# Padding that moves operand tiles of four product stages, and the first stage's turning of tiles put inside the product

## The chip, the cores and the metric

One Trainium2 chip; the kernel runs on one of its cores. The metric is the device time of one execution in microseconds (us). The kernel before was run three times: 4549.24, 4552.47 and 4555.07 us, median 4552.47. One execution was also profiled.

## The reference

Two transformer blocks of different build follow each other on 1024 tokens of width 1024, in float32. Only the dense products matter here; what stands between them (gated linear attention, windowed attention, retention, a delta rule, long convolutions) is left out.

```python
# first block
h = layer_norm(x) * (1.0 + scale1) + shift1
proj = h @ w_in[l]                                  # 1024 x 6416 weights
x = layer_norm_affine(ALPHA * x + gate1 * (y @ w_o[l]), ln1_g[l], ln1_b[l])
h2 = layer_norm(x) * (1.0 + scale2) + shift2
u = h2 @ w_up[l]                                    # 1024 x 5632
f = jax.nn.gelu(u_gate, approximate=False) * u_val
x = layer_norm_affine(ALPHA * x + gate2 * (f @ w_down[l]), ln2_g[l], ln2_b[l])
# second block, layer 0 (even), on 1024 tokens and 256 of context
u_l = h_l @ w_in                                    # 1024 x 4352
u_c = h_c @ w_in
# second block, layer 1 (odd)
u_l = h_l @ w_in                                    # 1024 x 4096
kv_c = h_c @ w_in[:, O_NK:O_NZ]
```

## The kernel before

The program is a chain of stages, in this order: g_in (first projection, with windowed attention and the modulation rows woven in), gla, proj1, up, down, g_even, ret, prep, rwkv, proj2, g_odd, mix, proj3. Each stage (`stage`, L44) gives back its memory and semaphores at its end. Within a stage each engine has its own instruction stream, written out by hand; semaphores tie them together.

Every float32 product is done as three products of rounded parts: each operand is split into a high part (an ACT copy into F32R) and a low part (a DVE subtraction), and high x high, high x low and low x high are summed in PSUM. One product instruction has a stationary operand of 128x128 and a moving one of 128x512 (the last strip is narrower). In g_in, g_even and g_odd the helper `gemm_units` (L84) does it: a unit is one strip of 512 weight columns times one tile of 128 tokens, 8 chunks of 128 input features x 3 = 24 matmuls (`multiply`, L139; L151 to L153); activations `hi`, `lo` are stationary, weights `w_hi`, `w_lo` moving. Weight chunks are loaded by SP's queue into `raw`, a ring of 4 (`load`, L118), split by ACT (L131) and DVE (L137) into a ring of `slots` chunks, and the last four chunks of the next strip wait for the last unit of this one. PSUM has two banks, emptied by ACT and DVE in turn (L167, L173), and POOL's queue stores the results (L178). In up (L1592) it is the other way round: weights stationary, activations moving, 22 column blocks x 96 matmuls. In down (L1835 to L1839) the activations `f_hi`, `f_lo` are stationary and the weights moving; blocks of 36 matmuls (24 in the last pass) take their weights in turn from three places: for two of three blocks from spare columns of `hi`, `lo` (shown as h_hi, h_lo), for the third from `w_hi2`, `w_lo2` (shown as down_w_hi, down_w_lo). In the proj stages (L468 to L470) activations `y_hi` are stationary and weights moving.

A memory tile of a stage stands right behind the one opened before it, rounded up to 32 bytes of each partition; so shapes give every tile's place. The 128x128 identity comes first (512 bytes), then the activations of the stage. Counted within 512 bytes from the identity's first byte, the operands of the products stand at:

| stage | activations | weights | tiles in between whose size is no multiple of 512 bytes |
|---|---|---|---|
| g_in | 0 | 0 | none |
| proj1 | 96 | 96 | (`mod_cols1`, 96 bytes, before both) |
| up | 0 | 288 | `mod_cols1` 96, `taps` 704 |
| down, two blocks of three | 192 | 0 | `mod_cols` 192, before f_hi |
| down, third block | 192 | 192 | |
| g_even | 0 | 192 | `mod_cols` 192 |
| proj2 | 192 | 192 | |
| g_odd | 0 | 192 | `mod_cols2` 192 |
| proj3 | 0 | 0 | |

The start of g_in. `in_order` (L1086) is run by every engine with its own functions. A tile of x is loaded by POOL's queue into one of two buffers (`x_in`, L1075), its moments are taken and it is scaled into `xn` by DVE (`norm`, L1382 to L1398, with ACT's square root L1348 in between); PE turns it with eight 128x128 transposes into `pt` (L1273); ACT scales and shifts it from `pt` into `h` (eight activations, L1357) and copies the high part (L1360); DVE subtracts for the low part (L1411). There is one `xn`, one `pt` and one `h`, so the tiles go through one at a time. The order is norm(0), norm(1), turn_in(0), and then for each unit u: norm(u+2), turn_in(u+1), unit(u), the attention steps from unit 24 on and the modulation rows from unit 4 on. Unit u waits for the low part of tile u (`h_lo`, L1286 to L1287); the transposes of tile u+1 stand ahead of unit u on PE and wait until ACT has emptied `pt` of tile u. Before that, PE sums the first eight modulation blocks (L1259) as their loads land, and DVE makes `cols` from them (L1403 to L1408) right after the low parts of the first eight weight chunks.

Of the kernel before, what the change touches and what calls it, by code (L numbers as in the profile page):

```python
# [17 lines left out]
P = 128  # L18
# [51 lines left out]
RAW = 4  # L70
# [13 lines left out]
def gemm_units(s, sb, ps, hi, lo, w, strips, plan, slots=12):  # L84
# [3 lines left out]
    raw = sb("g_raw", [P, RAW, width])  # L88
# [50 lines left out]
    def multiply(pe, u):  # L139
# [6 lines left out]
        for k in range(KC):  # L146
            c = st * KC + k
# [868 lines left out]
def in_stage(nc, ident, t_eye, padded, src, w_first, b_first, w_in, P1, pos, sinks, t_mask, t_first, t_freq, YB, conds, mods):  # L1016
# [5 lines left out]
    with stage(nc, "g_in", "id_in", "zero", "pad_out", "c_in", "c_silu", "f0", "f1", "f2", "f3", "f4", "f5", "f6", "f7", "bias_T", "row_mm", "rows", "cond", "silu", "rows_in", "cols_T", "cols", "in_even", "in_odd", "var", "std", "xn", "in_T", "h", "h_hi", "h_lo",  # L1022
# [52 lines left out]
        x_in = sc[:].rearrange("p a h k -> p a (h k)")  # L1075
# [10 lines left out]
        def in_order(norm, turn_in, unit, step, mod):  # L1086
# [24 lines left out]
        def _(sp):  # L1111
# [48 lines left out]
            in_order(lambda t: None, lambda t: None, unit, step, mod)  # L1160

        @block.gpsimd
        def _(pool):
            def load_in(t):
                if t >= 2:
                    pool.wait_ge(s.xn, t - 1)
                if t < NT:
                    pool.dma_start(x_in[:, t % 2], src[t * P:(t + 1) * P, :]).then_inc((s.in_even, s.in_odd)[t % 2], DMA)
            load_in(0)
            load_in(1)  # L1170
# [23 lines left out]
            in_order(lambda t: load_in(t + 1) if t else None, lambda t: None, unit, step, mod)  # L1194
# [6 lines left out]
        def _(pe):  # L1201
# [61 lines left out]
            def turn_in(t):  # L1263
# [21 lines left out]
            def unit(u):  # L1285
# [4 lines left out]
                gemm.multiply(pe, u)  # L1290
# [9 lines left out]
            in_order(lambda t: None, turn_in, unit, step, mod)  # L1300

        @block.scalar
        def _(act):
# [42 lines left out]
            def norm(t):  # L1346
                act.wait_ge(s.var, t + 1)
                act.activation(rstd[:, 0:1], rstd[:, 1:2], ACT.Sqrt).then_inc(s.std, 1)  # L1348

            def turn_in(t):  # L1350
                act.wait_ge(s.in_T, t + 1)
                if t == 0:
                    act.wait_ge(s.cols, 1)
                else:
                    act.wait_ge(s.h_lo, t)
# [17 lines left out]
            def first(t):  # L1373
                norm(t)
                if t == 1:
                    for c in range(KC):
                        gemm.split_hi(act, c)
# [2961 lines left out]
```

## Time and profile before

| | us |
|---|---|
| median of three runs | 4552.47 (4549.24 to 4555.07) |
| the profiled execution | 4550.96 |
| its span from first to last instruction | 4549.2 |
| PE busy with matmuls | 4064.8 (89%) |
| DVE busy | 2600.8 (57%) |
| ACT busy | 1481.1 (33%) |
| mean granted TensorE clock | 0.936 |

The sections below read the same trace in more detail. A duration of a matmul holds its fill and drain and overlaps the next one; what a matmul costs in a stream is the distance from one start to the next. Times in the trace count from the span's start.

### The profile page before, as it was taken

Reading aid. Unit: us, or ns where it says so; the run is one execution under the profiler, and the core shown is the slowest. Engines: PE = TensorE matmul, PEld = TensorE weight load, DVE = VectorE, ACT = ScalarE, POOL = GpSimd, SP = SyncE. Lnnn points to the kernel's source line nnn. Section 1 sums busy time; section 2 is a strip of 40 time slices with the busy share of each in tenths; the row PEclk is TensorE's granted clock in tenths of the full one; section 3 lists DMA queues with packets and bytes.
Section 4 is the critical chain, followed back from the end, with each engine's and each line's share of the span. In section 5 each row is a group of like instructions: output and inputs, shape, how many; then the busy total and the mean of one; then the engine's idle time right before and its main releaser. Section 6 shows DMA issues by size and latency. Waiting matters only on the chain. (4 is left out here: it accounts for less than half of the span.)

```text
span 4549.2 us, 71258 instructions
## 1 busy us (share of the span) xinstructions
PE 4064.8 (89%) x27486; PEld 3117.6 (69%) x27486; DVE 2600.8 (57%) x4923; ACT 1481.1 (33%) x3051; POOL 614.4 (14%) x802
## 2 busy tenths in 40 slices
PE   6999999768999989799997577899968999989988
PEld 4877776557888877588886233788766778755647
DVE  4567775667333348711237686777765335465746
ACT  4223232734222235411104243334433311143423
POOL 1111111000000000010123012000010013333320
PEclk8999999889999999899997688999878999999999
DMA  6544433542111144522323585444434335453334
GB/s 203 185 149 138 160 128 112 182 145 92 46 46 47 36 134 154 165 94 86 116 105 113 171 304 205 122 115 133 113 98 151 134 117 193 162 159 97 105 97 158
DMA packets 422564, 599.56 MB, mean 132 GB/s; under 512 B 166703, under 2 KB 279811, under 8 KB 419621
## 3 DMA queue, kind: packets, MB, share of 16 engines
q1 hardware_dynamic: 369037, 417.99, 29.8%
q0 software_dynamic: 51120, 174.80, 10.5%
q8 instruction: 204, 3.34, 0.3%
q10 hardware_dynamic: 2088, 2.49, 0.2%
q14 instruction: 115, 0.94, 0.1%
HBM read 430.45 MB, written 164.71 MB: 131 GB/s over the span
## 5 line engine op out<-in xcount | busy, mean ns | idle before, releaser
L151 PE MATMUL g_in_g_acc<-g_in_g_whi,g_in_hi 128*128 128x512 f32 (+1 forms) x832 | 328.7, 395 | 5.7 <-DVE g_in_lo L1411 5.7
L152 PE MATMUL g_in_g_acc<-g_in_g_wlo,g_in_hi 128*128 128x512 f32 (+1 forms) x832 | 319.0, 383 | 0.0
L153 PE MATMUL g_in_g_acc<-g_in_g_whi,g_in_lo 128*128 128x512 f32 (+1 forms) x832 | 318.6, 383 | 0.0
L151 PE MATMUL g_even_g_acc<-g_even_g_whi,h_hi 128*128 128x512 f32 (+1 forms) x720 | 276.4, 384 | 12.4 <-DVE g_even_g_wlo L137 12.4
L152 PE MATMUL g_even_g_acc<-g_even_g_wlo,h_hi 128*128 128x512 f32 (+1 forms) x720 | 275.7, 383 | 0.0
L153 PE MATMUL g_even_g_acc<-g_even_g_whi,h_lo 128*128 128x512 f32 (+1 forms) x720 | 275.5, 383 | 0.0
L1668 DVE SCALAR_TENSOR_TENSOR rows<-up_acc,up_taps,rows 128x1023 f32<-128x1023 f32 x88 | 112.8, 1282 | 284.4 <-ACT rows L1643 277.1
L1592 PE MATMUL up_acc<-h_hi,up_w_hi 128*128 128x512 f32 x704 | 225.6, 397 | 13.1 <-DVE up_w_lo L1682 11.1
L151 PE MATMUL g_odd_g_acc<-g_odd_g_whi,h_hi 128*128 128x512 f32 x544 | 218.5, 402 | 17.0 <-DVE g_odd_g_wlo L137 11.4
L1592 PE MATMUL up_acc<-h_lo,up_w_hi 128*128 128x512 f32 x704 | 225.3, 397 | 0.0
L1592 PE MATMUL up_acc<-h_hi,up_w_lo 128*128 128x512 f32 x704 | 225.1, 397 | 0.0
L152 PE MATMUL g_odd_g_acc<-g_odd_g_wlo,h_hi 128*128 128x512 f32 x544 | 216.7, 398 | 0.0
L153 PE MATMUL g_odd_g_acc<-g_odd_g_whi,h_lo 128*128 128x512 f32 x544 | 216.6, 398 | 0.0
L1436 DVE SCALAR_TENSOR_TENSOR g_in_m_acc<-g_in_m_w,g_in_c_act,g_in_m_acc 128x256 f32<-128x256 f32 x448 | 202.0, 482 | 22.3 <-issue 0.4
L151 PEld LDWEIGHTS g_in_g_acc<-g_in_g_whi,g_in_hi 128*128 128x128 f32 x832 | 156.5, 188 | 66.0 <-issue 26.0
L468 PE MATMUL proj_acc<-proj_w_hi,proj_y_hi 128*128 128x512 f32 x416 | 170.7, 410 | 15.2 <-DVE proj_w_lo L543 15.2
L153 PEld LDWEIGHTS g_in_g_acc<-g_in_g_whi,g_in_lo 128*128 128x128 f32 x832 | 156.6, 188 | 31.5
L152 PEld LDWEIGHTS g_in_g_acc<-g_in_g_wlo,g_in_hi 128*128 128x128 f32 x832 | 156.8, 188 | 27.4
L1643 ACT ACTIVATE rows<-up_acc,up_taps 128x1024 f32<-128x1024 f32 x44 | 53.1, 1206 | 372.1 <-PE up_acc L1592 372.1
L470 PE MATMUL proj_acc<-proj_w_hi,proj_y_lo 128*128 128x512 f32 x416 | 166.1, 399 | 0.0
L469 PE MATMUL proj_acc<-proj_w_lo,proj_y_hi 128*128 128x512 f32 x416 | 166.0, 399 | 0.0
L151 PEld LDWEIGHTS g_even_g_acc<-g_even_g_whi,h_hi 128*128 128x128 f32 x720 | 135.7, 188 | 43.6 <-DVE g_even_g_wlo L137 14.0
(640 smaller groups left out, 9450.8 us busy)
## 6 DMA issues: line engine op xcount, KB each, us to landing
rest<-in_w_down SPq DMA_DIRECT2D x66, 512.0 KB, 3.6
g_in_g_raw<-in_w_in SPq DMA_DIRECT2D x96, 256.0 KB, 4.1
P<-g_in_g_o POOLq DMA_DIRECT2D x96, 256.0 KB, 2.7
g_in_m_w<-in_ada_w SPq DMA_DIRECT2D x24, 1024.0 KB, 5.4
up_w_buf<-in_w_up SPq DMA_DIRECT2D x42, 512.0 KB
U<-g_even_g_o POOLq DMA_DIRECT2D x80, 256.0 KB, 2.3
g_odd_x<-U3p SPq DMA_DIRECT2D x24, 768.0 KB, 6.9
g_in_m_w<-in_w_ada SPq DMA_DIRECT2D x16, 1024.0 KB, 6.4
```

Of the source, the lines that this page charges most:

```text
L151: pe.matmul(bank[:, :wd], hi[:, k, tt], w_h, start=k == 0, stop=False)
L152: pe.matmul(bank[:, :wd], hi[:, k, tt], w_l, start=False, stop=False)
L153: op = pe.matmul(bank[:, :wd], lo[:, k, tt], w_h, start=False, stop=k == KC - 1)
L468: pe.matmul(acc[t % 2][hf][:], y_hi[:, t % 2, k, :], w_hi[:, k, cs], start=k == 0, stop=False)
L469: pe.matmul(acc[t % 2][hf][:], y_hi[:, t % 2, k, :], w_lo[:, k, cs], start=False, stop=False)
L470: op = pe.matmul(acc[t % 2][hf][:], y_lo[:, t % 2, k, :], w_hi[:, k, cs], start=False, stop=k == KC - 1)
L1436: dve.scalar_tensor_tensor(acc, w, c_act[:, k, c:c + 1], acc, ALU.mult, ALU.add)
L1592: op = pe.matmul(acc[par][side][:, tt], wt[:, par, side, k, :], ht[:, k, tt], start=k == 0 and wt is w_hi and ht is hi, stop=k == KC - 1 a ...
L1643: act.activation(cv[:, side], acc[par][side][:], ACT.Identity, scale=taps[:, 2, col], bias=taps[:, 3, col]).then_inc(s.act_c, 1)
L1668: dve.scalar_tensor_tensor(cv[:, side, lag:], acc[par][side][:, :SEQ - lag], taps[:, tap, col], cv[:, side, lag:], ALU.mult, ALU.add)
```

## The change

Four edits of memory layout and one of order. (1) `gemm_units` takes `pad`; `raw` gets `width + pad` columns per chunk. g_even and g_odd pass 20, so `raw` is 4 x 20 x 4 = 320 bytes longer. (2) `taps` in up gets 14 more columns in each of its 4 rows, 224 bytes. (3) down opens an unused tile `place` of 320 bytes ahead of `f_hi`. With these the operands of up, down, g_even and g_odd stand at the same place within 512 bytes (0, 0, 0 and 0). The chunks of `raw` then begin 2128 bytes apart in place of 2048. (4) In g_in the turning of tile u+2 moves into unit u, after 12 of its 24 matmuls (`middle`); x tiles have three buffers (the third is `y`, unused so early) and `norm` is cut in `moments` and `scale`, run one and two tiles further ahead; the moments of tile 2 come ahead of the making of `cols`, and POOL issues the loads of tiles 0 to 2 at once, tile 3 after the scaling of tile 0, tiles 4 and 5 ahead of the first store.

```diff
-def gemm_units(s, sb, ps, hi, lo, w, strips, plan, slots=12):
+def gemm_units(s, sb, ps, hi, lo, w, strips, plan, slots=12, pad=0):
-    raw = sb("g_raw", [P, RAW, width])
+    raw = sb("g_raw", [P, RAW, width + pad])
...
-    def multiply(pe, u):
+    def multiply(pe, u, middle=None):
...
         for k in range(KC):
+            if k == KC // 2 and middle:
+                middle()
...
-        x_in = sc[:].rearrange("p a h k -> p a (h k)")
+        x_in = [sc[:, 0].rearrange("p h k -> p (h k)"), sc[:, 1].rearrange("p h k -> p (h k)"),
+                y[:].rearrange("p h d -> p (h d)")]
+        x_done = (s.in0, s.in1, s.in2)
...
-            norm(0)
-            norm(1)
-            turn_in(0)
+            for what, t in (("moments", 0), ("scale", 0), ("moments", 1), ("scale", 1), ("chunks", 0), ("moments", 2), ("turn", 0), ("low", 0),
+                            ("turn", 1), ("scale", 2), ("moments", 3), ("low", 1)):
+                early(what, t)
             for u in range(gemm.units):
-                if u + 2 < NT:
-                    norm(u + 2)
-                if u + 1 < NT:
-                    turn_in(u + 1)
+                for what, t in (("turn", u + 2), ("scale", u + 3), ("moments", u + 4), ("low", u + 2)):
+                    if t < NT:
+                        early(what, t)
                 unit(u)
...
             def load_in(t):
-                if t >= 2:
-                    pool.wait_ge(s.xn, t - 1)
-                if t < NT:
-                    pool.dma_start(x_in[:, t % 2], src[t * P:(t + 1) * P, :]).then_inc((s.in_even, s.in_odd)[t % 2], DMA)
-            load_in(0)
-            load_in(1)
+                if t >= 3:
+                    pool.wait_ge(s.xn, t - 2)
+                pool.dma_start(x_in[t % 3], src[t * P:(t + 1) * P, :]).then_inc(x_done[t % 3], DMA)
+            for t in range(4):
+                load_in(t)
...
-            in_order(lambda t: load_in(t + 1) if t else None, lambda t: None, unit, step, mod)
+            in_order(lambda what, t: load_in(t + 3) if what == "scale" and 1 <= t < NT - 3 else None, unit, step, mod)
...
-                gemm.multiply(pe, u)
+                gemm.multiply(pe, u, (lambda: turn(u + 2)) if u + 2 < NT else None)
...
-            in_order(lambda t: None, turn_in, unit, step, mod)
+            in_order(lambda what, t: turn(t) if what == "turn" and t < 2 else None, unit, step, mod)
...
+            def early(what, t):
+                if what == "moments":
+                    act.wait_ge(s.var, t + 1)
+                    act.activation(rstd[:, 0:1], rstd[:, 1:2], ACT.Sqrt).then_inc(s.std, 1)
+                if what == "chunks":
+                    for c in range(KC):
+                        gemm.split_hi(act, c)
...
+                if what == "low":
+                    act.activation(hi[:, :, rows(t * P)], h, ACT.Copy).then_inc(s.h_hi, 1)
...
-        taps = sb("taps", [P, 4, 2 * FC])
+        taps = sb("taps", [P, 4, 2 * FC + 14])
...
-                dve.tensor_copy(taps[:, c, :], acc[1][0][:, c * P:c * P + 2 * FC])
+                dve.tensor_copy(taps[:, c, :2 * FC], acc[1][0][:, c * P:c * P + 2 * FC])
...
+        sb("place", [P, 80])
         f_hi = sb("f_hi", [P, W_BUF, 384], F32R)
...
-        gemm = gemm_units(s, sb, ps, hi, lo, w_in, EVEN_STRIPS, plan)
+        gemm = gemm_units(s, sb, ps, hi, lo, w_in, EVEN_STRIPS, plan, pad=20)
...
-        gemm = gemm_units(s, sb, ps, hi, lo, w_in, ODD_STRIPS, plan, slots=10)
+        gemm = gemm_units(s, sb, ps, hi, lo, w_in, ODD_STRIPS, plan, slots=10, pad=20)
```

ACT's and DVE's functions of the first stage are cut along the same names; `turn` keeps the eight activations L1357, `low` has the copy L1360 and the subtraction L1411, `scale` has L1391 to L1398, `moments` L1384 to L1390.

## Rows read from the trace of the kernel before

**Rows 1.** Busy time by stage: length, busy us per engine, clock, DMA share, GB/s.
```profile
1610.00:1895.00 285.00, 256.89 (x1120) 207.54 (x1120) 198.39 (x378) 134.18 (x285) 11.75 (x17) 0.97 0.51 158
1895.00:2395.00 500.00, 482.62 (x2178) 391.45 (x2179) 126.33 (x205) 68.57 (x122) 73.77 (x134) 0.98 0.31 106
3570.00:3985.00 415.00, 397.08 (x1657) 312.09 (x1657) 163.84 (x143) 65.23 (x109) 112.90 (x101) 0.98 0.46 161
```

**Rows 2.** The same view, PE alone: within g_even, g_odd, up.
```profile
1940.00:2300.00 360.00, 360.00 (x1544) 1.00 0.29 98
3750.00:3880.00 130.00, 130.00 (x559) 1.00 0.55 195
1130.00:1600.00 470.00, 470.00 (x2016) 1.00 0.15 43
```

**Rows 3.** Timeline of PE in g_in: start, length, operation; 29 and 23 distances.
```profile
101.04 0.39 PE L152 MATMUL g_in_g_acc<-g_in_g_wlo,g_in_hi 128*128 128x512 f32 x1
...
107.64 0.39 PE L151 MATMUL g_in_g_acc<-g_in_g_whi,g_in_hi 128*128 128x512 f32 x1
...
112.85 0.39 PE L153 MATMUL g_in_g_acc<-g_in_g_whi,g_in_lo 128*128 128x512 f32 x1
```

**Rows 4.** Timeline of PE in proj2; 24 distances lie between the two.
```profile
3465.74 0.39 PE L468 MATMUL proj_acc<-proj_w_hi,proj_y_hi 128*128 128x512 f32 x1
...
3471.18 0.39 PE L468 MATMUL proj_acc<-proj_w_hi,proj_y_hi 128*128 128x512 f32 x1
```

**Rows 5.** Timeline of PE in down: between the rows 17 and 36 distances.
```profile
1624.97 0.39 PE L1836 MATMUL down_acc<-down_w_lo,down_f_hi 128*128 128x512 f32 x1
...
1628.82 0.40 PE L1835 MATMUL down_acc<-h_hi,down_f_hi 128*128 128x512 f32 x1
...
1637.08 0.40 PE L1835 MATMUL down_acc<-down_w_hi,down_f_hi 128*128 128x512 f32 x1
```

**Rows 6.** Timeline of PE, narrow strips: g_even (46 distances), g_in (29).
```profile
2359.83 0.28 PE L151 MATMUL g_even_g_acc<-g_even_g_whi,h_hi 128*128 128x256 f32 x1
...
2365.04 0.28 PE L152 MATMUL g_even_g_acc<-g_even_g_wlo,h_hi 128*128 128x256 f32 x1
...
154.26 0.29 PE L152 MATMUL g_in_g_acc<-g_in_g_wlo,g_in_hi 128*128 128x272 f32 x1
...
157.90 0.29 PE L151 MATMUL g_in_g_acc<-g_in_g_whi,g_in_hi 128*128 128x272 f32 x1
```

**Rows 7.** Timeline of PE in g_in: units 0, 1, 3 and transposes.
```profile
47.41 0.79 PE L151 MATMUL g_in_g_acc<-g_in_g_whi,g_in_hi 128*128 128x512 f32 x1 [0.37 <-DVE g_in_lo L1411]
...
54.59 1.03 PE L1273 MATMUL g_in_pt<-ident,g_in_pT 128*128 128x128 f32 x8
55.38 0.47 PE L151 MATMUL g_in_g_acc<-g_in_g_whi,g_in_hi 128*128 128x512 f32 x1
...
70.72 0.50 PE L151 MATMUL g_in_g_acc<-g_in_g_whi,g_in_hi 128*128 128x512 f32 x1 [1.24 <-DVE g_in_lo L1411]
...
77.21 1.06 PE L1273 MATMUL g_in_pt<-ident,g_in_pT 128*128 128x128 f32 x8 [0.76 <-ACTq L1358]
```

**Rows 8.** Groups by line, 0:111: count, busy us, mean ns, idle before.
```profile
L1357 ACT ACTIVATE g_in_pT<-g_in_pt,g_in_cols 128x128 f32<-128x128 f32 x64 | 23.2, 467 | 4.3 <-DVEq L1408 2.9 <-DVE g_in_lo L1411 1.4
L1411 DVE TENSOR_TENSOR g_in_lo<-g_in_pT,g_in_hi 128x1024 fp32r<-128x1024 f32 x8 | 9.8, 1225 | 23.7 <-ACT g_in_hi L1360 23.7
L1360 ACT ACTIVATE g_in_hi<-g_in_pT 128x1024 fp32r<-128x1024 f32 x8 | 8.5, 1058 | 0.8
```

**Rows 9.** Timeline of DVE around the first unit.
```profile
39.77 0.68 DVE L1403 COPY g_in_x<-g_in_pm 128x512 f32<-128x512 f32 x1
...
47.28 1.28 DVE L1386 BATCH_NORM_STATS2 g_in_stats<-g_in_sc 128x6 f32<-128x512 f32 x2
...
48.93 0.15 DVE L1390 TENSOR_SCALAR g_in_rstd<-g_in_mv 128x1 f32<-128x1 f32 x1
```

**Rows 10.** Busy time of 20:40; columns as in rows 1.
```profile
20.00:40.00 20.00, 6.87 (x32) 0.76 (x32) 8.00 (x16) 4.74 (x9) 7.01 (x10) 0.59 1.02 309
```

More of the change, by code:

```diff
@@ L1159, in _ @@
                 gemm.load(sp, c)
-            in_order(lambda t: None, lambda t: None, unit, step, mod)
+            in_order(lambda what, t: None, unit, step, mod)
         @block.gpsimd
@@ L1371, in unit, with moments @@
                 gemm.evacuate_act(act, u)
[L1373 to L1377, printed above, removed]
-            in_order(lambda t: first(t) if t < 2 else norm(t), turn_in, unit, step, lambda m: None)
+            in_order(early, unit, step, lambda m: None)
         @block.vector
         def _(dve):
-            def norm(t):
-                xt = x_in[:, t % 2]
-                dve.wait_ge((s.in_even, s.in_odd)[t % 2], (t // 2 + 1) * DMA)
+            def moments(t):
+                dve.wait_ge(x_done[t % 3], (t // 3 + 1) * DMA)
                 for hf in range(2):
-                    dve.bn_stats(stats[:, hf, :], xt[:, hf * 512:(hf + 1) * 512])
+                    dve.bn_stats(stats[:, hf, :], x_in[t % 3][:, hf * 512:(hf + 1) * 512])
                 dve.drain()
@@ new lines, in early @@
+            def early(what, t):
+                if what == "moments":
+                    if t == 0:
+                        dve.memset(zeros, 0.0).then_inc(s.zero, 1)
+                    if t == 1:
+                        dve.wait_ge(s.bias_T, 1)
+                        dve.tensor_copy(cols[:], bias_T)
+                    moments(t)
+                if what == "scale":
+                    scale(t)
+                    if t == 0:
+                        dve.memset(ones[:], 1.0)
+                if what == "chunks":
+                    for c in range(KC):
+                        gemm.split_lo(dve, c)
+                if what == "turn" and t == 0:
+                    columns()
+                if what == "low":
+                    dve.wait_ge(s.h_hi, t + 1)
+                    dve.tensor_tensor(lo[:, :, rows(t * P)], h, hi[:, :, rows(t * P)], ALU.subtract).then_inc(s.h_lo, 1)
@@ L1524, in unit @@
                 gemm.evacuate_dve(dve, u)
-            def first(t):
-                if t == 0:
-                    dve.memset(zeros, 0.0).then_inc(s.zero, 1)
-                if t == 1:
-                    dve.wait_ge(s.bias_T, 1)
-                    dve.tensor_copy(cols[:], bias_T)
-                norm(t)
-                if t == 0:
-                    dve.memset(ones[:], 1.0)
-                if t == 1:
-                    for c in range(KC):
-                        gemm.split_lo(dve, c)
-            in_order(lambda t: first(t) if t < 2 else norm(t), turn_in, unit, step, mod)
+            in_order(early, unit, step, mod)
 def ffn_up_stage(nc, ident, hi, lo, left, cols, X1, cv, w_up, conv_w, conv_b, fT):
```

54 lines of the change are left out of this document (24 added, 30 removed).

## The prediction

> **What bounds the kernel now.** I began with the busy time by stage. In down, g_even and g_odd PE works 257 of 285, 483 of 500 and 397 of 415 us, DVE 198, 126 and 164, and the DMA share is 0.51, 0.31 and 0.46 [rows 1]. Inside them and inside up the same view shows stretches of 360, 130 and 470 us in which PE has no gap at all, at a granted clock of 1.00, which is the 2.4 GHz level [rows 2]. So these stages last as long as PE needs for their matmuls, and a change in the distance from one matmul to the next goes straight into the end. The length printed at a matmul (0.39) is no help there, as it overlaps the next; the distance is a stretch divided by its matmuls.
>
> That distance is not the same in all stages. Of the count in a stretch one or two only reach into it. g_even: 360 us over 1543 is 233.3 ns; up: 470 over 2015 is 233.3; g_odd: 130 over 558 is 233.0 [rows 2]. g_in needs 5.21 us for 23, 226.5 ns, and 11.81 us for 29 + 23 = 52, 227.1, over a stretch that has a few slower distances in it [rows 3]. proj2 needs 5.44 for 24, 226.7 [rows 4]. The table of places orders them: g_in and proj2 have both operands at one place within 512 bytes (0 and 0, 192 and 192), the slow three are 192 or 288 bytes apart. It is the distance of the places and not the weights' own place: in proj2 and in g_even the weights stand at 192 alike. Nor is it the roles, since up has them exchanged. Down has both kinds in one stage, with the same instructions: its third block, both operands at 192, needs 3.85 us for 17, 226.5, and the following 36 matmuls, 192 bytes apart, 8.26 us, 229.4 [rows 5]. That is the strongest row for the change, and also a warning: in down the price of being apart is 2.9 and not 6.7 ns.
>
> **Part 1, the places.** Nothing is added to any engine; 320, 224, 320 and 320 bytes of memory are. I take 227.1 as the distance after, the value with slower distances in it, and 233.3 before, so 6.2 ns a matmul; 6.8 would be the bound above (233.3 to 226.5), 0 the bound below unless the rival decides.
> - g_even: 8 strips of 512 columns x 10 token tiles x 24 = 1920 matmuls x 6.2 = 11.9 us.
> - g_odd: 68 units x 24 = 1632 x 6.2 = 10.1 us.
> - up: 22 x 96 = 2112 x 6.2 = 13.1 us.
> - down: 22 x (18 + 18 + 12) = 1056 x (229.4 - 227.1) = 2.4 us. The third blocks gain as well, because the row at 226.5 is the first of its kind and later ones start out of a block that is apart; but in the last two passes DVE is close behind (198 busy of 285 over the stage) [rows 1], so I take 1.5.
> - g_even's last strip has 256 columns: 240 matmuls. Apart they need 5.21 us for 46, 113.3 ns. The nearest row at one place is g_in's strip of 272: 3.64 us for 29, 125.5, or 118.1 for 256 columns in proportion [rows 6]. So the narrow strip may lose 240 x 4.8 = 1.2 us; I take all of it. Its bound below is 0.
>
> Sum 11.9 + 10.1 + 13.1 + 1.5 - 1.2 = 35.4 us. It is on the path since PE is the bound; the cover of the other engines is large (DVE 126 of 500 in g_even). What is late next in each stage is what is late now: the first weight chunks at its start.
>
> The rule of the Trainium skill that speaks against this is in "TensorE: Matmul & The Clock Gate", Part 2, step 1 of the walk through a matmul: loading the next stationary operand "doesn't steal SBUF read bandwidth from the running matmul", as each has its own read port. By it the place could not matter and part 1 would be worth 0. The rows disagree, as the same instruction form runs at 226.5 and at 229.4 in one stage [rows 5]; still it is a rival below. The same page's figure for a matmul of 512 columns in a row, about 216 ns, is under every row here, so both levels carry a cost that it lacks.
>
> The chunks of `raw` now begin at multiples of 16 bytes that are no multiples of 64. The trace shows no DMA to such a place. Its bound below is a gain of 0, since nothing in it gets shorter; above, if each load took half as long again, only the first chunks of g_even and g_odd would show, some 2 us each; later chunks are loaded a strip ahead and a strip lasts 56 or 45 us. I take 0 and keep 4 in the range.
>
> **Part 2, the first stage.** Removed from the path: the wait for `h_lo` ahead of units 3, 4, 5 and 6 and the wait for `pt` ahead of transposes, 1.24 and 0.76 at the rows shown [rows 7], and the drains and starts around them. Kept: the transposes themselves, 0.79 us from 54.59 to 55.38, and a slower first matmul behind each (0.47 to 0.50 against 0.39) [rows 7], about 0.1. Eight units now take 47.41 to 107.64, 60.2 us [rows 7, 3]. After: unit 0 has its first matmuls at the lower clock level as now (0.79 long against 0.39) [rows 7]: from 47.41 to 54.59 are 7.2, plus 0.8 and some 0.1 for transposes: 8.1. Units 1 to 5: 24 x 0.2268 = 5.44, plus 0.9: 6.35 each, 31.8. Units 6 and 7 hold no transposes: 10.9. Sum 50.8, so 9.4 less.
>
> This holds if the chain of the other engines fits in a unit of 6.35. ACT needs 2.9 for the eight activations and 1.06 for the copy, DVE 1.2 for the low part [rows 8], 5.2 in a row per tile, since `h` is single; beside them DVE takes the moments (1.8) [rows 9] and the scaling, which it does while ACT works. Before unit 4 this leaves about a unit's length as slack, because the low part of tile u+2 is due only after unit u+1. From unit 4 on DVE has the modulation rows as well, but no more moments. The tightest places are the transposes in unit 4 and the start of unit 5, with about 1 us each by this count; a miss costs what it misses, up to 2 us.
>
> Two things are moved ahead of the first unit. The moments of tile 2 stand between the last weight chunk and the making of `cols` on DVE: 47.28 to 49.08 is 1.8 us for the same work [rows 9]. Behind them in DVE's queue is L1403, now right at the chunk's end (39.77) [rows 9], for which PE, ACT and so the first unit wait. So +1.8. And POOL's queue issues the loads of x tiles 2 to 4 before that point, where tile 4 (0.5 MB) came behind the first unit's store before; the DMA engines are full there (share 1.02 between 20 and 40 us, 309 GB/s) [rows 10], so the last weight chunk lands later by 0.5 MB over 309 GB/s, 1.7 us. I take that; the bounds are 0 and 3, as earlier loads of tiles 2 and 3 could also hold up tile 1 and the first chunks. POOL's constants behind these loads are due much later. SP's loads of modulation weights stand behind a chunk that DVE splits after the low part of tile 3, some 5 us later than now, and are wanted only in unit 4.
>
> Sum of part 2: 9.4 - 1.8 - 1.7 = 5.9 us, from 2 to 9.5. From unit 8 on the stage runs as before, PE without waits, so the shift goes through.
>
> **The sum.** The profiled execution took 4551.0 with a span of 4549.2, 1.5 under the median of the runs. 4551.0 - 35.4 - 5.9 = 4509.7, stated as 4510; were the median of its runs 1.5 above it again, it would be 4511.
>
> **The rivals.**
> - Only part of the places helps. Down shows 2.9 ns where the others show 6.7, so what decides may be a pattern of places and order, and up (moving activations, each stationary tile used twice) has no sister at one place. Without up: 4510 + 13 = 4523; with half the gain everywhere, 4528. Against it: four streams at one place, in three stages and two shapes of loop, all give 226.5 to 227.1.
> - The places do nothing (the rule above, or the distance comes of something else that these stages share, such as the longer rows of `hi` in g_even and g_odd). Then part 2 alone is left: 4551 - 6 = 4545, and it is "the same" by the bound below. Against it: up has the short rows and is slow; down has both in one stage.
> - Slower: at one place the load of the stationary tile and the stream collide, and the 226.7 of g_in comes from elsewhere. Being apart would be the better place, as it is in the narrow strips (118 against 113 ns) [rows 6]. If the wide ones lost the same 4.8 ns, 6720 matmuls x 4.8 = 32 us, less 6: 4577. It decides if the loss sits in the load of 128 columns whatever the stream's width. Against it: proj2's and g_in's wide streams.
> - The first stage gives nothing because the start comes later than counted: 4510 + 6 = 4516, inside the range.
>
> **How the numbers follow.** Forecast, including a first stage of 2 to 9.5: 0.83. Part of the places: 0.08. Nothing: 0.05. Slower: 0.03; a mixture between nothing and slower: 0.01. Faster by over 0.2% (9 us, about what a measurement of this kernel can tell from no change) is 0.92 with a share of the partial cases, the same 0.05, slower 0.03. Low end: 6.8 in place of 6.2 ns (3.4 us), no loss in the narrow strip (1.2), 9.5 in the first stage (3), less a little: 4502. High end: 2 in the first stage (4), 4 for `raw`, and up to the partial cases: 4524.
>
> **What would show it.** In the changed profile the stretches of g_even, g_odd and up should hold 2.8% more matmuls each (360 us: 1587 and not 1544); up's stage should end 13 us sooner after its start; down's blocks of all three kinds should run at 226.5 to 227.5. Unit 0 of g_in should start at 51, unit 8 at 102, with no wait for L1411 between. Wrong would be: a distance still at 233 with both operands at one place; PE waits for `w_lo` at strip changes; L1403 later than 43.

## The result, and the profile after

The changed kernel took 4517.9 us in the median of four executions (4514.4 to 4523.1), the kernel before beside it 4552.9 (4549.2 to 4555.1): a ratio of 0.9923, 95% interval 0.9908 to 0.9939. It is faster by about 35 us; forecast were 41, counted from the profiled execution of 4551.0. The time lies inside the range of 4502 to 4524 and 8 us above the forecast of 4510. The profiled execution took 4514.4 us with a span of 4512.6, which is 36.6 less than the span before, at the same mean granted clock (0.937 and 0.936).

Stage by stage, from the first matmul of a stage to its last:

| stage | before | after | change | forecast |
|---|---|---|---|---|
| g_in, to its end | 778.4 | 772.8 | -5.6 | -5.9 |
| up | 498.8 | 485.1 | -13.7 | -13.1 |
| down | 274.2 | 272.1 | -2.1 | -1.5 |
| g_even | 488.7 | 477.0 | -11.7 | -10.7 |
| g_odd | 403.9 | 399.0 | -4.9 | -10.1 |
| all the rest, by difference | | | +1.4 | 0 |

The view of PE alone in stretches without a gap answers to [rows 2]; columns as there.

```profile
1920.00:2280.00 360.00, 360.00 (x1590) 1.00 0.31 104
1120.00:1580.00 460.00, 460.00 (x2031) 1.00 0.16 44
3860.00:3930.00 70.00, 70.00 (x311) 1.00 0.44 155
```

g_even holds 1590 matmuls in 360 us where it held 1544: 360 / 1589 = 226.6 ns. up: 460 / 2030 = 226.6. g_odd: 70 / 310 = 225.8, one matmul more or less being 0.7 ns. So the distances came down by the full 6.7 ns and not by the 6.2 of the forecast. Counted from unit to unit, each unit of 24 matmuls is 0.16 us shorter, in g_even's wide strips from the fifth unit on and in up from the second of its 22 column blocks on without exception.

The narrow strip went the other way. Timeline of PE in g_even after, 46 distances between the two, against 5.21 us for as many before [rows 6]: 5.52 us, 120.0 ns.

```profile
2325.58 0.28 PE L156 MATMUL g_even_g_acc<-g_even_g_whi,h_lo 128*128 128x256 f32 x1
...
2331.10 0.28 PE L154 MATMUL g_even_g_acc<-g_even_g_whi,h_hi 128*128 128x256 f32 x1
```

The start of g_in, timelines of PE and of DVE, against [rows 7] and [rows 9]:

```profile
42.81 1.12 PE L1285 MATMUL g_in_pS<-ident,g_in_x 128*128 128x128 f32 x4 [6.07 <-DVE g_in_x L1405]
...
49.70 0.79 PE L154 MATMUL g_in_g_acc<-g_in_g_whi,g_in_hi 128*128 128x512 f32 x1 [0.37 <-DVE g_in_lo L1432]
...
100.53 0.39 PE L154 MATMUL g_in_g_acc<-g_in_g_whi,g_in_hi 128*128 128x512 f32 x1
```
```profile
38.49 1.95 DVE L138 TENSOR_TENSOR g_in_g_wlo<-g_in_g_raw,g_in_g_whi 128x512 fp32r<-128x512 f32 x3 [0.47 <-ACT g_in_g_whi L132]
40.36 1.28 DVE L1387 BATCH_NORM_STATS2 g_in_stats<-g_in_y 128x6 f32<-128x512 f32 x2
...
42.07 0.68 DVE L1405 COPY g_in_x<-g_in_pm 128x512 f32<-128x512 f32 x1
```

Unit 0 starts at 49.70 and not 47.41, unit 8 at 100.53 and not 107.64: eight units in 50.83 us. The 7.11 us won by then are still there to 0.01 at unit 76; at unit 80 they are 5.54. In between the granted clock fell to the lower level for about 3.4 us, which shows as a mean of 0.89 in this stretch, beside 1.00 in the same one before (PE busy, clock, DMA share, GB/s; before is the first):

```profile
560.00:575.00 15.00, 13.43 (x81) 1.00 0.41 158
```
```profile
560.00:575.00 15.00, 13.43 (x79) 0.89 0.26 89
```

And g_odd has a wait that was nearly absent before. Waits of PE there, 3700 to 3960 before, then 3700 to 3920 after (total, times, longest):

```profile
PE g_odd_g_acc L151 <- DVE g_odd_g_o L173: 5.6, 1, 5.6
PE g_odd_g_acc L151 <- DVE g_odd_g_wlo L137: 1.1, 1, 1.1
```
```profile
PE g_odd_g_acc L154 <- DVE g_odd_g_o L176: 5.5, 2, 5.3
PE g_odd_g_acc L154 <- DVE g_odd_g_wlo L138: 4.3, 1, 4.3
```

The second line, the wait for `w_lo`, is in the first unit of a strip, at its seventh matmul. Counted from 0 as in g_in this is unit 52; the expectations below call it unit 53. Ahead of it nearly every unit of g_odd is 0.16 us shorter than before; across it 4.5 us of that are lost: 3.2 in the longer wait, the rest in matmuls at the lower clock level right behind it (the clock is 0.89 over 3845:3860 and 1.00 over the 70 us after).

### The profile page after: what moved, and what is told of

Its sections match the earlier page's. It is cut to its first block and busy times, and to the rows that moved or that the text cites. A ratio compares the mean times of both kernels' runs of the same rounds, so it can differ in the third digit from the quotient of the medians.

```text
span 4512.6 us, 71257 instructions
## 1 busy us (share of the span) xinstructions
PE 4035.5 (89%) x27486; PEld 3123.9 (69%) x27486; DVE 2607.0 (58%) x4923; ACT 1480.6 (33%) x3051; POOL 614.2 (14%) x802
## 5 line engine op out<-in xcount | busy, mean ns | idle before, releaser
L154 PEld LDWEIGHTS g_even_g_acc<-g_even_g_whi,h_hi 128*128 128x128 f32 x720 | 136.4, 189 | 39.0 <-DVE g_even_g_wlo L138 14.1
```

What stands on the lines that cost most here:

```text
L154: pe.matmul(bank[:, :wd], hi[:, k, tt], w_h, start=k == 0, stop=False)
```

## Where the wait in g_odd comes from

DVE runs the convolution of a tile between its other duties. In the last unit of a strip (unit 51 here) its queue holds the low parts of the next strip's last six weight chunks: six and not four as in g_in and g_even, because g_odd's ring has ten places. A tile's first product stands ahead of them. Timelines of DVE and of POOL after, then the same place before:

```profile
3846.36 1.82 DVE L3655 SCALAR_TENSOR_TENSOR g_odd_x<-g_odd_x,g_odd_edges,g_odd_w 128x1536 f32<-128x1536 f32 x1 [10.16 <-DMA g_odd_x<-U3p]
3848.25 5.55 DVE L138 TENSOR_TENSOR g_odd_g_wlo<-g_odd_g_raw,g_odd_g_whi 128x512 fp32r<-128x512 f32 x4
3846.41 5.04 POOL L3587 TENSOR_TENSOR g_odd_x<-g_odd_x,g_odd_w 128x1536 f32<-128x1536 f32 x1 [4.00 <-DMA g_odd_x<-U3p]
```
```profile
3880.60 1.82 DVE L3645 SCALAR_TENSOR_TENSOR g_odd_x<-g_odd_x,g_odd_edges,g_odd_w 128x1536 f32<-128x1536 f32 x1 [6.13 <-DMA g_odd_x<-U3p]
3882.49 5.65 DVE L137 TENSOR_TENSOR g_odd_g_wlo<-g_odd_g_raw,g_odd_g_whi 128x512 fp32r<-128x512 f32 x4
3880.84 4.94 POOL L3577 TENSOR_TENSOR g_odd_x<-g_odd_x,g_odd_w 128x1536 f32<-128x1536 f32 x1
```

The same work of the same length; but unit 52, the first that needs these low parts, started at 3884.77 before and at 3846.19 after. So x landed 4.2 us ahead of that unit before, and 0.2 behind its start after. DVE stands in the wait for x with the low parts behind it. A second delay follows from the same landing: POOL starts its own product of the tile then, and the first of the four low parts (one row above) takes 3.75 us beside it (3.84 before) where the others take 0.68. It ends at 3852.00, and PE's wait at 3852.05. Before, this delay was as long, but the low parts had started early enough to hide most of it. Without it PE would have waited about 1.2 us and not 4.3, by an estimate from 3.75 and 0.68. The timeline of SP says why x is late in terms of units: its loads are issued when DVE has finished the tile before,

```profile
3871.06 1.27 SPq L3529 DMA_DIRECT2D g_odd_x<-U3p  x3
```
```profile
3835.17 1.28 SPq L3539 DMA_DIRECT2D g_odd_x<-U3p  x3
```

which is 13.7 us ahead of unit 52 before and 11.0 after, and they took 9.5 us from issue to DVE's release before and 11.2 after. The chain finish, load, first product has its own length in us; the steps that hold it are counted in units, and the units became shorter. Each tile's load waits for the tile before, so the lag adds up over the tiles. That was the reading of the two traces; the runs below test it.

## The experiments

Ratios are against the kernel before on the same chip. Distances are the mean of all start-to-start distances of a stage's wide matmuls under 300 ns, unless a row is shown; in down they are those of the two blocks of three whose relative place the padding changes. Line numbers of each kernel are its own.

**Each part alone.** The first kernel is the kernel before with the padding only, the second the changed kernel without it (the line is that of g_even and g_odd; `taps` in up and `place` in down likewise):

```diff
-        raw = sb("g_raw", [P, RAW, width])
+        raw = sb("g_raw", [P, RAW, width + 20])
```

> The kernel before with only the memory padding of up, down, g_even and g_odd, the first stage untouched. Theory A (the distance between matmuls is set by the places of the two operands within 512 bytes, 233.3 ns apart and 226.7 at one place, whatever the first stage does): every unit of 24 matmuls is 0.16 us shorter, up 14 us shorter, g_even 11, down 2, g_odd 11 less a wait for w_lo at a strip change of 4, in all 31 to 34 us: 4519 to 4522. Rival B (part of the gain of these stages comes of the shifted start of everything, that is of the moments at which loads and clock changes fall): under 25 us, 4528 or more.

Measured: 4524.6 us against 4556.4, ratio 0.9934 (0.9918 to 0.9951), 32 us less, which is inside theory A's 31 to 34 and far from rival B's 25. up 486.2 long, down 272.4, g_even 477.5, g_odd 400.8, all within 2 us of the changed kernel; g_in as before.

> The changed first stage alone, all tiles at their former places. Theory A: unit 0 of g_in starts near 49.7 and unit 8 near 100.5, 7.1 us ahead of before, and all later stages run at 233.3 ns as before; 7 us less, or 5.5 if the clock falls once within g_in as it did in the changed kernel: 4545 to 4547. Rival: the clock's fall near 565 us is an accident of one execution and is not seen here (then 4545); or it follows from the earlier start (then the fall is there again at 560 to 570).

Measured: 4545.7 against 4556.4, ratio 0.9980 (0.9971 to 0.9990), 11 us less by the medians; in its trace unit 8 of g_in starts at 100.74 and the stage ends at 771.5, 6.9 us ahead of before, all of it kept, since the clock did not fall inside the stage. up, g_even and g_odd run at 233.3 ns. The parts add up within their intervals: 0.9934 x 0.9980 = 0.9914, against 0.9923 for both. Waits of PE in g_odd, with the padding alone and with the first stage alone:

```profile
PE g_odd_g_acc L151 <- DVE g_odd_g_wlo L137: 5.6, 1, 5.6
```
```profile
PE g_odd_g_acc L154 <- DVE g_odd_g_wlo L138: 0.4, 1, 0.4
```

The wait at the strip change goes with the padding and not with the earlier start. It remains to tell the shorter units from raw's odd places.

**raw at multiples of 2048 again.**

```diff
-    raw = sb("g_raw", [P, RAW, width + pad])
+    if pad:
+        sb("g_place", [P, 80])
+    raw = sb("g_raw", [P, RAW, width])
```

> The changed kernel, but the 320 bytes in g_even and g_odd are an unused tile ahead of raw, so that raw's chunks are 2048 bytes apart as before and not 2128; the operands stand at the same places as in the changed kernel. Theory A (the odd places of raw's chunks cost nothing; the wait for w_lo at the strip change in g_odd comes of DVE standing in a wait for a tile of the convolution): g_odd keeps its wait of 3 to 5 us at unit 53, total as the changed kernel, 4517 within 2. Rival B (loads to places that are no multiples of 64 bytes, or reads from them, are slower and cause that wait): the wait is gone or under 1.5 us and the total is 3 to 5 us less, 4513.

Measured: 4520.1, ratio 0.9919 (0.9903 to 0.9936). The wait is there in full:

```profile
PE g_odd_g_acc L156 <- DVE g_odd_g_wlo L140: 5.4, 1, 5.4
```

So raw's places cost nothing that these runs can tell, rival B falls, and the 4 us kept for them above the forecast were not needed.

**DVE's first convolution product one step later.**

```diff
-                if n == 0:
+                if n == 1:
                     dve.wait_ge(s.const, 5 * DMA)
                     dve.wait_ge(s.x_in, (t + 1) * (3 * DMA))
                     dve.scalar_tensor_tensor(before, before, edges[:, 0, t:t + 1], w[:, 0], ALU.mult, ALU.mult)
                     dve.drain()
-                if n == 1:
                     dve.scalar_tensor_tensor(behind, behind, edges[:, 1, t:t + 1], w[:, 2], ALU.mult, ALU.mult)
```

> The changed kernel, with one change in g_odd: DVE does the first product of a convolution tile (the one that waits for the three loads of x) one step later, together with the second, so that some 3.6 us more lie between the loads' issue and the wait. Theory A (the new wait of PE at unit 53 is DVE's queue: it stands in the wait for x, 10.16 us there, and the low parts of the next strip's last four chunks stand behind it): DVE no longer waits there, PE's wait of 4.34 goes under 1, g_odd ends 3 to 4.4 us sooner, 4513.5 to 4515 on the scale on which the changed kernel is 4517.9. Rival B (the low parts are late because POOL multiplies beside them, 4.4 us for one in place of 0.69): POOL still starts when x has landed, so a wait of 2 to 4 us stays.

Measured: 4511.9, ratio 0.9902 (0.9884 to 0.9919); g_odd 392.4 us long instead of 399.0 and, in a second execution of the changed kernel, 399.9. Timeline of DVE at the same strip change:

```profile
3843.23 2.73 DVE L138 TENSOR_TENSOR g_odd_g_wlo<-g_odd_g_raw,g_odd_g_whi 128x512 fp32r<-128x512 f32 x4 [6.11 <-ACT g_odd_g_whi L132]
3849.86 2.20 DVE L138 TENSOR_TENSOR g_odd_g_wlo<-g_odd_g_raw,g_odd_g_whi 128x512 fp32r<-128x512 f32 x2 [3.90 <-ACT g_odd_g_whi L132]
3851.98 0.68 DVE L176 COPY g_odd_g_o<-g_odd_g_acc 128x512 f32<-128x512 f32 x1
3852.59 1.80 DVE L3655 SCALAR_TENSOR_TENSOR g_odd_x<-g_odd_x,g_odd_edges,g_odd_w 128x1536 f32<-128x1536 f32 x1
```

The low parts come at their time, the convolution behind them without a wait. PE's waits in 3700:3920:

```profile
PE g_odd_g_acc L154 <- DVE g_odd_g_wlo L138: 3.8, 5, 1.6
PE g_odd_g_acc L154 <- DVE g_odd_g_o L176: 2.4, 2, 1.9
```

At unit 52 PE now waits 0.2 us for low parts and not 4.3, as theory A has it (under 1). Theory A's 3 to 4.4 us for the stage were too small: the wait of 5.3 us for `g_odd_g_o`, which is in the kernel before too (5.6), had the same cause (in the changed kernel's trace DVE waits 12.01 us for the first tile's x, with the emptying of a PSUM bank behind it) and shrinks to 1.9. But the edit moves waits too: 3.6 of the 3.8 us above stand in the first units of strips that had no wait before (units 34, 44 and 60). The two kinds together are 6.2 us where they were 9.8; the clock gives the rest, a mean of 0.98 over these 220 us in the changed kernel and of 1.00 here. In the three later kernels that hold this edit the waits sum to 6.2 to 6.6 us.

Rival B expected a wait of 2 to 4 us to stay at unit 52, and none did. Yet the run doesn't clear POOL: the edit takes the low parts out of the wait for x and out of POOL's product at once, as they are done at 3845.96 and POOL starts at 3847.41. Four low parts took 5.55 us beside POOL's product and 2.73 here. So that DVE's wait for x is what made the wait of PE grow is shown, since POOL's delay was in the kernel before too; how the 4.3 us divide between the two is read from the trace alone. No run leaves DVE's product in its place and moves POOL's.

**Which places are good.** Three kernels with other paddings, raw unpadded. A number is the place of the moving operand less that of the stationary one within 512 bytes; the edit is the size of the padding only.

> The changed kernel with other places: moving minus stationary operand within 512 bytes is 192 in g_in (0 in the changed kernel), 256 in g_even, 64 in g_odd, 128 in up and 64 in two of three blocks of down. Theory A1 (only the same place within 512 bytes is fast): all five run at 233.3, g_in loses 15 us over 96 wide units. Theory A2 (the same place within 256 bytes is enough, as of two halves): g_even at 226.7, the others at 233.3. Theory A3 (within 64 bytes): refuted already, since 192 is slow; if 64 or 128 were fast here the distance would count and not the place within a row. g_in at 192 must become slow by every theory that has the place as the cause; if g_in stays at 226.7, the cause lies in the other stages' code.

> More places, moving minus stationary within 512 bytes: 32 in g_in, 384 in g_even, 320 in g_odd, 96 in up, 192 in two blocks of three of down. Theory A (what counts is the difference within 256 bytes, with a cost that grows from 0 at 0 over 2.4 ns at 64 and 5.7 at 128 to 6.7 at 192): g_even at 384 runs as at 128, 232.4; g_odd at 320 as at 64, 229.1; g_in at 32 near 228; up at 96 near 231; down at 192 near 233. Theory B (256 is a second good place, but within 512 each difference has its own cost): g_odd at 320 or g_even at 384 differ by over 1 ns from that.

> More places, moving minus stationary within 512 bytes: 160 in g_in, 32 in g_even, 448 in g_odd, 256 in up and 256 in two blocks of three of down. Theory A (difference within 256 bytes): up and down run at 226.7 to 227.3 as at one place; g_odd at 448 as at 192, 233.3; g_even at 32 near 228; g_in at 160 near 233. Theory B as in the run before: up at 256 slow, since its stationary operands are the weights, or g_odd at 448 off by over 1 ns. For the narrow strip of 256 columns, 120.0 ns at a difference of 0 and 256 and 113.4 at 192, theory A gives a value in between at 32.

Measured, with the kernels before and after for 0, 192, 224 and down's 320 (g_in's means hold the work between its matmuls: 228.2 at one place, so 5.0 to 6.0 are the price there). The three kernels ran once each, 4543.5, 4552.4 and 4545.1 us; their distances are what counts here:

| difference within 512 | within 256 | ns per wide matmul |
|---|---|---|
| 0 | 0 | up, g_even 226.7; g_odd 227.0; down 227.2; g_in 228.2 |
| 256 | 0 | up, g_even 226.7; down 227.1 |
| 32 | 32 | g_even 233.3; g_in 233.2 |
| 64 | 64 | g_odd 229.1; down 229.4 |
| 320 | 64 | g_odd 230.0; down 229.6 |
| 96 | 96 | up 233.4 |
| 128 | 128 | up 232.4 |
| 384 | 128 | g_even 232.4 |
| 160 | 160 | g_in 234.2 |
| 192 | 192 | g_even, g_odd, g_in, down 233.3 |
| 448 | 192 | g_odd 233.4 |
| 224 | 224 | up 233.4 |

The stretches without a gap, PE alone (in g_even's rows of the first two kernels the products only, without the transposes that fall into them). Difference 256 in g_even, 128 in up (first kernel):

```profile
1940.00:2300.00 360.00, 359.37 (x1586) 1.00 0.30 101
1130.00:1590.00 460.00, 460.00 (x1981) 1.00 0.15 45
```

384 in g_even, 96 in up (second); 32 in g_even, 256 in up (third):

```profile
1940.00:2300.00 360.00, 359.37 (x1547) 1.00 0.28 98
1130.00:1590.00 460.00, 460.00 (x1974) 1.00 0.16 45
```
```profile
1940.00:2300.00 360.00, 360.00 (x1545) 1.00 0.30 102
1130.00:1590.00 460.00, 460.00 (x2031) 1.00 0.17 46
```

What follows. The place is the cause: g_in, fast before and after, became slow when its weights were set 192 bytes off, with its code unchanged; it took 777.0 us and not 765, of which about 1.6 are a fall of the clock. The same place within 256 bytes is enough: 256 is as good as 0 in three stages, 384 equals 128, 448 equals 192, and 320 equals 64 within 1 ns (230.0 and 229.1 in g_odd, just under theory B's bound of 1). The price does not grow with the difference, as theory A of the second and third kernel had it: 32 costs the full 6.7, 64 only 2.4 to 3.3, 128 again 5.7. The two roles are alike (up has its weights stationary). And the wait for low parts in the last part of g_odd goes with the length of a unit: at 233.3 and 233.4 ns 1.1, 0.4 and 0, at 230.0 1.1, at 229.1 2.5, at 227.0 4.3 to 5.6 us.

One thing in the kernel before doesn't fit a price that is set by the place alone. In down the third block of three (18 matmuls; the 36 of [rows 5] are two blocks) has both operands at one place, and the prediction read 226.5 ns from the first of them. The other 21 took 227.4 to 231.3 in the mean, as the second, timeline of PE before:

```profile
1637.08 0.40 PE L1835 MATMUL down_acc<-down_w_hi,down_f_hi 128*128 128x512 f32 x1
...
1639.40 0.62 PE L1839 MATMUL down_acc<-down_w_hi,down_f_lo 128*128 128x512 f32 x2
...
1641.21 0.40 PE L1835 MATMUL down_acc<-h_hi,down_f_hi 128*128 128x512 f32 x1
```

The first ten distances take 2.32 us, 232 ns each, the last eight 1.81 us, 226 each. So behind a block whose operands stand apart, a stream at one place needs about ten matmuls to reach its level; where PE had waited just before, it needed fewer in most cases. With all blocks at one place, in the changed kernel, 15 of 22 third blocks run at 226.6 to 226.7 from their first distance on. The sweeps gave all blocks of up, g_even and g_odd one place, so their means don't hold this.

**The moments of tile 2 behind the making of cols.**

```diff
-("chunks", 0), ("moments", 2), ("turn", 0), ("low", 0),
+("chunks", 0), ("turn", 0), ("moments", 2), ("low", 0),
```

> The changed kernel, with the moments of tile 2 behind the making of cols and not ahead of it. Theory A (unit 0 is late by these 1.7 us on DVE): DVE takes the sums at 40.4 instead of 42.07, unit 0 starts at 48.0 instead of 49.70 and everything behind it 1.7 us sooner; DVE then works on the moments while ACT makes h, and nothing waits for them. Rival B (the modulation sums on PE are not ready before 42, so that the moments cost nothing): start unchanged at 49.7. Rival C: the moments then push the low part of tile 0, start at 49 or later.

Its profiled execution took 12321 us at a mean granted clock of 0.41, which nothing in this edit explains and no other run shows, so its trace isn't used. The timed ones took 4511.6 to 4520.5, ratio 0.9907 (0.9887 to 0.9927), which doesn't tell 1.7 us from nothing. The edit is read from the next kernels, which hold it too.

**The changed kernel again, and three edits together.** The third edit, in `gemm_units`, moves a narrow strip's weights within their chunk:

```diff
+    def cols_of(wd):
+        at = 48 if wd < width else 0
+        return slice(at, at + wd)
...
-            w_h, w_l = w_hi[:, c % slots, :wd], w_lo[:, c % slots, :wd]
+            w_h, w_l = w_hi[:, c % slots, cols_of(wd)], w_lo[:, c % slots, cols_of(wd)]
```

> The changed kernel once more, beside the next one on the same chip, to see which of the differences between two executions belong to the kernel. Theory A: distances, the wait of PE at unit 53 of g_odd (4 to 5.5 us) and unit 0 of g_in at 49.7 come again; the fall of the clock inside g_in at 565 us does not, so that g_in ends 1.6 us sooner, at 771. Ratio to the kernel before 0.992.

Measured: 4520.2, ratio 0.9927 (0.9913 to 0.9940), span of the profiled execution 4512.7. Unit 0 at 50.02, unit 8 at 100.14, g_in's end at 770.8 and no fall of the clock within it; the wait at the strip change in g_odd is 5.4. All as expected.

> The changed kernel with three edits that each undo a loss seen in it: DVE's first convolution product one step later in g_odd, the moments of tile 2 behind the making of cols, and the last, narrow strip's weights 192 bytes on within their chunk in gemm_units (g_even's 256 columns, g_in's 272). Theory: g_odd 4 to 6.5 us shorter; unit 0 of g_in at 48.0 and not 49.7, in all 1.7; the narrow strip of g_even back at 113.4 ns and not 120.0, 240 x 6.6 = 1.6 us, g_in's 272 columns at 123.4 and not 125.3, 192 x 1.9 = 0.4. Sum 8 to 10 us less than the changed kernel, ratio to the kernel before 0.990. Rivals: without the moments' share (unit 0 stays at 49.7 because PE's sums are late anyway) 6.5 to 8.5; if the narrow strip's place does not decide its distance, it stays at 120.0.

Measured: 4509.0, ratio 0.9902 (0.9887 to 0.9916), 11 us less than the changed kernel beside it by the medians and 7.4 by the profiled spans. g_odd is 393.9 long, 6.0 less, which is most of it. Timelines of DVE and PE at g_in's start:

```profile
39.26 1.97 DVE L141 TENSOR_TENSOR g_in_g_wlo<-g_in_g_raw,g_in_g_whi 128x512 fp32r<-128x512 f32 x3 [0.27 <-ACT g_in_g_whi L135]
41.14 0.69 DVE L1408 COPY g_in_x<-g_in_pm 128x512 f32<-128x512 f32 x1
```
```profile
48.87 0.80 PE L157 MATMUL g_in_g_acc<-g_in_g_whi,g_in_hi 128*128 128x512 f32 x1 [0.46 <-DVE g_in_lo L1435]
```

The sums follow the last chunk at once, so the 1.7 us between them are gone as theory A of the moments has it; but the chunk itself is 0.8 us later in this execution, so that unit 0 starts 0.8 to 1.2 sooner and not 1.7 (48.87 here, 48.68 and 48.70 in the two kernels below). g_in ends no earlier (770.9), because the clock fell for 3.4 us at 702, which costs the 1.6 us again. And the narrow strip disappoints: g_in's 272 columns run at 123.4 as expected, g_even's 256 at 117.8 and not 113.4. As late_step alone has the same ratio, 0.9902, the times can't tell whether the other two edits are worth anything.

**The narrow strip.** Two kernels ask why. In the first `at` is 176 (704 bytes) and not 48. In the second the narrow strips are not moved; all of g_in's weights stand 512 bytes further on, and g_even's 512 bytes further than in the kernel before.

> As the kernel with the three edits, but the narrow strip's weights stand 704 bytes on within their chunk and not 192: the same place within 512 bytes, another within 1024. There the 256 columns took 117.8 ns at 192 bytes and not the 113.4 of the kernel before, whose weights stood 192 within 512 from the activations too, but 512 bytes elsewhere within 1024. Theory A (for a narrow stream the place within 1024 bytes counts): 113.4 here, g_even 1.1 us shorter. Theory B (what the distance settles into depends on the strips before it, which ran at one place here and apart in the kernel before): 117.8 again.

> The three-edit kernel without the shift of the narrow strips; instead all weights of g_in stand 512 bytes further on (difference 0 within 512) and those of g_even 512 bytes further than in the kernel before (difference 192). Theory for the wide strips: only the place within 256 bytes counts, so g_in's wide ones keep 228.2 in the mean with what is between them and g_even's run at 233.3. For the narrow strip of g_even, theory A (place within 1024 bytes): 117.8; theory B (the strips before it): 113.4 as in the kernel before, since wide strips apart go before it here as there.

Measured, as 46 distances of the narrow strip each, timelines of PE in g_even of the first and of the second: 5.42 us, 117.8 ns; 5.22 us, 113.5 ns.

```profile
2329.97 0.28 PE L159 MATMUL g_even_g_acc<-g_even_g_whi,h_lo 128*128 128x256 f32 x1
...
2335.39 0.28 PE L157 MATMUL g_even_g_acc<-g_even_g_whi,h_hi 128*128 128x256 f32 x1
```
```profile
2343.04 0.28 PE L158 MATMUL g_even_g_acc<-g_even_g_whi,h_lo 128*128 128x256 f32 x1
...
2348.26 0.28 PE L156 MATMUL g_even_g_acc<-g_even_g_whi,h_hi 128*128 128x256 f32 x1
```

Theory A, the place within 1024 bytes, is refuted twice. Both results agree with theory B, that the distance depends on the strip before it (apart: 113.4; at one place: 117.8 with its own weights apart, 120.0 with them at one place). Two earlier kernels speak against it in this simple form. In the third kernel of the sweep all of g_even stood 32 bytes apart, wide strips (233.3) and narrow one alike, and the narrow one took 117.8; its expectation had asked for a value between 113.4 and 120.0. The second kernel, 128 bytes apart within 256, gave 118.7. And g_in's 272 columns, 192 bytes apart, took the same 125.7 in the mean behind wide strips at one place (the three edits) and behind wide strips 192 bytes apart (first kernel of the sweep), against 127.6 at one place. What a strip takes over from what ran before is seen in down, above, but there it is gone after ten matmuls; what sets the narrow strips' distance stays open. The wide strips did as their theory says: g_in 228.2 with the 512 bytes, g_even 233.3. The first kernel took 4513.9, ratio 0.9906 (0.9889 to 0.9922), the second 4523.1 in one execution. Neither is better than the three edits with 48 (0.9902), nor are those better than late_step alone (0.9902).

## Why the prediction held, and where it was off

- The distance is set by the relative place, in every stage and both roles: right, and shown by g_in's loss at 192 bytes. What in the chip makes the difference no run here shows. The size was a little low. I took 227.1 for the distance after, a value with slower distances in it; it is 226.7, so 6.67 ns a matmul and not 6.2. up 88 x 0.16 = 14.1 (13.1 taken), g_even 80 x 0.16 = 12.8 (11.9), g_odd 68 x 0.16 = 10.9 before its wait (10.1).
- Down. The row called the strongest, 226.5 in the third block, was the one such block of 22 in its stage that ran so; the others give 227.4 to 231.3 with the same places. The forecast took this into account ("later ones start out of a block that is apart"), but as evidence for the place the row was luck; what carries the claim is g_in. The warning row, 229.4 in place of 233.3 [rows 5], has its reason: 320 bytes apart is 64 within 256, and 64 is a half-good place in g_odd too (229.1, 230.0). 2.1 us came, of 1.5 taken and 2.4 possible.
- The rule of the Trainium skill in "TensorE: Matmul & The Clock Gate", Part 2, step 1, that loading the next stationary operand takes no read bandwidth from the running matmul: the runs disagree with what the prediction drew from it, that the place could not matter, with a mean of 228.2 and 233.3 ns for the same instructions in g_in according to the weights' place alone.
- The narrow strip: the sign was right, from a neighbour of 272 columns; the size 1.6 us in place of 1.2.
- raw at 16-byte places: nothing, as taken.
- First stage: eight units took 50.83 us, forecast 50.8. Unit 0 started at 49.70, forecast 50.9. The 1.8 for the moments was nearly right (42.07 - 40.44 = 1.6 between the last chunk and the sums); the 1.7 for the loads of tile 4 was too much here (0.6: the last low part ended at 40.44 and not at 39.85), though in other executions with this order it was 0.9 to 1.7. By unit 8 it gave 7.1 and not 5.9.
- The step that failed is the one on what is late next: "what is late next in each stage is what is late now: the first weight chunks at its start". In g_odd it was DVE's queue, standing in the wait for x with the next strip's low parts behind it, and then POOL's product beside the first of them. I named a PE wait for `w_lo` at strip changes as a sign of a wrong forecast and gave raw as the only way to it; the row was in the profile before, as a wait of 1.1 us at one strip change, and I had not asked what it hung on. It cost 4.5 us of the 10.9. The sum had this term at nothing.
- A fall of the clock in g_in, 1.6 us, was not in the sum either. The runs don't tie it to the change: the second profiled execution of the same kernel lacks it, and of all thirteen traces five have such a fall in g_in, at moments from 564 to 716 us, others with the same first stage none. The two traces with the old first stage have none either, which is too few to tell.
- The sum. Terms as measured: 14.1 + 2.1 + 12.8 - 1.6 + 10.9 + 7.1 = 45.4. Less 4.5 for the wait, 1.6 for the clock, 1.4 for small losses at the starts and at two units of g_odd, 1.4 for the stages that the change doesn't touch: 36.5, and the spans differ by 36.6. The two terms of 1.4 are differences of stage lengths, so the agreement is no test. The terms that were forecast came to 4.1 more than forecast (45.4 against 41.3) and the losses that were not came to 8.9. These two errors have opposite signs, so that the gain in the spans is only 4.7 us off is in part luck; the rest of the 8 us is that the median lies 3.5 us above the profiled execution. The stages that the change doesn't touch scatter by themselves: rwkv took 590.8 to 596.6 us and ret 120.1 to 122.4 over the thirteen traces.
- Of the rivals, "only part of the places" had its mechanism half right, in that places other than the same can be good or half good, but not in this kernel's layout; "nothing" and "slower" are refuted for 512 columns. For 256 columns "slower" is true.

## What to carry to other kernels

Where a stage is a dense stream of matmuls, look at where the two operands begin relative to each other: here the same place within 256 bytes took 3% off the distance of a 512-column matmul, for a few hundred bytes of memory, while for 256 columns it added 6%, so each width is to be measured. When a change makes the pacing engine faster, list the waits of the other engines that are now covered by it, above all a wait that stands ahead of that engine's own supplies in an in-order queue: its length is in us and doesn't shrink. A wait of 1 us at one of several like places in the profile is such a thing before it grows, and moving the waiting instruction one step later made its stage about 6 us shorter here, though it brought new short waits at other strip changes.

## What the runs showed of the hardware that was not expected

- Places that differ by 256 bytes are as good as equal ones, 64 is half good (229.1 to 230.0 ns), 128 slightly better than the rest (232.4), and 32, 96, 160, 192 and 224 cost the full 6.7 ns or somewhat more.
- Four of the levels are multiples of 6.67 ns in the mean: 226.7 is 34 of them, 233.3 is 35, 120.0 is 18, 113.3 is 17. The 117.8, 118.7, 234.2 and 229 to 232 are no such multiples; their single distances alternate (117, 118 and 119 ns in g_even's narrow strip).
- The distance of a narrow strip with the same difference of places, 192 bytes, was 113.4 or 117.8 ns, each in two kernels or more, by something that stays open.
- A wide stream at one place that follows one 320 bytes apart took 232 ns for ten matmuls and 226 to 227 from then on.
- A chain of DVE's low parts took 5.55 us for four that began beside a POOL product of 1536 columns, and 2.73 without it. All of the difference is in the first, 3.75 us in place of 0.68, which ends 0.55 us after POOL's product.
